# Constants in two loads, vectors loaded by ScalarE, gate rows dealt over the tiles, and conv rows and squares ahead in the delta rule

## The reference, cut to what matters

```
mk, mv = rmsnorm(mem) @ w_ck, rmsnorm(mem) @ w_cv            # 256 x 2048 each
proj = rmsnorm(x) @ w_in          # [q | k | v | z_A | alpha | beta | u | z_B]
q, k, v = silu(short_conv(proj[qkv], width 4)); q, k = l2norm(q) / sqrt(128), l2norm(k)
beta, g = sigmoid(..), -exp(a_log) * softplus(alpha + dt_bias)
o, state = gated_delta_rule(q, k, v, g, beta)                # 8 heads of 128, chunked
o_a = rmsnorm(o) * silu(z_A);  o_b = pooling(u) * silu(z_B)
x = x + [o_a, o_b] @ w_out
x = x + attention(rmsnorm(x) @ w_cq, mk, mv) @ w_co;  y = rmsnorm(x)
```

## Time and profile before

| | us |
|---|---|
| runs | 1755.1 median, 1754.63 to 1756.45 (3 runs) |
| the profiled execution's own time | 1756.3 |
| its span | 1754.5 |
| TensorE busy | 1698.6 (97%) |
| VectorE, ScalarE, GpSimd busy | 767.5, 604.8, 145.8 |
| DMA | 225.06 MB, mean 128 GB/s |

### The profile page before, as it was taken

The page is one execution under the profiler, slowest core; times in us unless marked ns, Lnnn a source line. Parts: engine busy times, 40 slices in busy tenths (PEclk is TensorE's granted clock), DMA queues, the critical chain, the costliest instruction groups (busy, mean ns, idle before and its releaser), DMA issues.

```text
span 1754.5 us, 31473 instructions
## 1 busy us (share of the span) xinstructions
PE 1698.6 (97%) x13184; PEld 1573.0 (90%) x13184; DVE 767.5 (44%) x1296; ACT 604.8 (34%) x967; POOL 145.8 (8%) x159
## 2 busy tenths in 40 slices
PE   5999999999999999999999999999999999999997
PEld 4887898998989998999999999999999987499997
DVE  4666435756646556465333343233122143422222
ACT  4565433442543434425322222222212133322222
POOL 0000000121111111211100001111000000000110
PEclk9999999999999999999999999999999999999999
DMA  6787643231332332414233334444433386723422
GB/s 228 235 290 240 202 110 84 71 105 52 109 87 73 86 84 74 110 49 122 66 93 92 81 99 148 129 128 143 151 91 96 100 329 267 222 75 108 121 79 103
DMA packets 272251, 225.06 MB, mean 128 GB/s; under 512 B 9785, under 2 KB 238914, under 8 KB 266706
## 3 DMA queue, kind: packets, MB, share of 16 engines
q1 hardware_dynamic: 272178, 224.03, 41.9%
HBM read 199.07 MB, written 25.30 MB: 128 GB/s over the span
## 4 chain that ended last, share of the span: by engine, by line
PE 92%; ACT 3%; issue 2%; DMA 1%; DVE 1%; POOL 0%; SPq 0%; ACTq 0%; DVEq 0%; POOLq 0%
PE pj L273 64%; PE pj L437 10%; PE dk L2140 2%; PE pj L2159 1%; PE dk L353 1%; PE dk L2071 1%; PE dk L1155 1%; PE pj L2082 1%; PE dk L1690 1%; PE pj L2168 1%; PE dk L1161 1%; PE dk L726 1%; PE dk L1299 1%; PE dk L1320 1%; DMA out_dram<-yb 1%
## 5 line engine op out<-in xcount | busy, mean ns | idle before, releaser
L273 PE MATMUL pj<-a_hi,w_high 128*128 128x272 f32 x2560 | 552.8, 297 | 12.6 <-ACT st L868 6.6
L273 PE MATMUL pj<-a_hi,w_low 128*128 128x272 f32 x2560 | 530.0, 288 | 0.0
L273 PE MATMUL pj<-a_lo,w_high 128*128 128x272 f32 x2560 | 528.4, 288 | 0.0
L273 PEld LDWEIGHTS pj<-a_hi,w_high 128*128 128x128 f32 x2560 | 402.4, 189 | 26.6 <-issue 21.1
L273 PEld LDWEIGHTS pj<-a_lo,w_high 128*128 128x128 f32 x2560 | 402.8, 189 | 0.0
L273 PEld LDWEIGHTS pj<-a_hi,w_low 128*128 128x128 f32 x2560 | 400.4, 189 | 0.0
L257 DVE TENSOR_TENSOR w_low<-w_raw,w_high 128x2048 fp32r<-128x2048 f32 x96 | 219.8, 2289 | 360.7 <-ACT w_high L247 360.6
L247 ACT ACTIVATE w_high<-w_raw 128x2048 fp32r<-128x2048 f32 x96 | 183.3, 1910 | 52.2 <-PE pj L273 44.8
L273 PE MATMUL pj<-mix_lo,w_high 128*128 128x272 f32 x512 | 105.7, 287 | 0.0
L273 PE MATMUL pj<-mix_hi,w_high 128*128 128x272 f32 x512 | 105.7, 288 | 0.0
L273 PE MATMUL pj<-mix_hi,w_low 128*128 128x272 f32 x512 | 105.6, 287 | 0.0
(11 more groups left out here) (394 smaller groups left out, 1797.7 us busy)
## 6 DMA issues: line engine op xcount, KB each, us to landing
w_raw<-in_w_in_dram SPq DMA_DIRECT2D x48, 1024.0 KB, 6.0
w_raw_wide<-in_w_ck_dram SPq DMA_DIRECT2D x16, 1024.0 KB, 6.6
w_raw_wide<-in_w_cv_dram SPq DMA_DIRECT2D x16, 1024.0 KB, 5.7
w_raw<-in_w_out_dram SPq DMA_DIRECT2D x16, 1024.0 KB, 6.0
w_raw<-in_w_cq_dram SPq DMA_DIRECT2D x16, 1024.0 KB, 5.9
w_raw<-in_w_co_dram SPq DMA_DIRECT2D x16, 1024.0 KB, 6.1
xr<-xT_scratch SPq DMA_DIRECT2D x16, 272.0 KB, 6.3
x2T_scratch<-x SPq DMA_DIRECT2D x16, 272.0 KB, 5.4
```

The lines of the kernel that those rows point to most:

```text
L273: mm = pe.matmul(pj[:, 2 * (q % 2) + b, 0:n], wt[:, k, :], x(k, o, n), start=(k == 0 and m == 0), stop=(k == KT - 1 and m == 2))
```

## The change

The constants are laid out anew, so that the identity and two columns of biases (NFIRST = 136 columns) come first; they are one load, and the rest, without columns of its own for the biases, a second one behind the first weight tile. The seven vector loads are issued by ACT, behind its table load. In group 0 of stage mem bank 2 is turned ahead of the products, banks 3 to 7 at earlier units, cast and split of part 1 go ahead of taking banks 2 and 3, and ACT's casts of parts 2 and 3 go between the two banks of their part. The gate rows' products stand after step 9; part 1 moves from q = 0 to q = 1 on ACT and DVE. In act_delta the square is two instructions with a signal each, k's part first, which the norms wait for one by one; `zraw` is taken behind the squares and not at the end of the head before; `rows()` of q = 2 stands ahead of the level-64 copies.

```diff
-C_ID, C_ONE, C_INCL, C_OWN, C_UP = 0, 128, 256, 384, 416
+C_ID, C_EPS, C_LNQ, C_ONE, C_INCL, C_OWN, C_UP = 0, 128, 129, 136, 264, 392, 424
+NFIRST = C_ONE
...
         def sp_mem(sp):
             sp.dma_start(xin[0][:], t["mem_prompt"][0, 0:P, :]).then_inc(x_loaded, 16)
-            sp.dma_start(cst[:], t["consts"][:, 0:NCONST]).then_inc(const_loaded, 16)
+            sp.dma_start(cst[:, 0:NFIRST], t["consts"][:, 0:NFIRST]).then_inc(const_loaded, 16)
             sp.dma_start(xin[1][:], t["mem_prompt"][0, P:MEM, :]).then_inc(mem1_loaded, 16)
-            for name, o, n in (("norm_mem", G_MEM, 16), ("norm_mix", G_MIX, 16), ("norm_cross", G_CROSS, 16),
...
-            sp.dma_start(vrow[0:NCONV, 1, :], t["conv_w"].rearrange("o j (k p) -> (o j k) p", p=P)).then_inc(vec_loaded, 16)
             for q in range(3):
                 sp.dma_start(raw_wide[q][:], source("mem", 0, q)).then_inc(w_loaded[q], 16)
+                if q == 0:
+                    sp.dma_start(cst[:, NFIRST:NCONST], t["consts"][:, NFIRST:NCONST]).then_inc(ab_loaded, 16)
...
             turn_mem(1)(pe)
+            turn_mem(2)(pe)
...
-                        if q < 3:
-                            steps = {2: [turn_mem(2 * q + 2)], 7: [turn_mem(2 * q + 3)]}
+                        steps = ({1: [turn_mem(3)], 7: [turn_mem(4)]}, {1: [turn_mem(5)], 6: [turn_mem(6)]},
+                                 {1: [turn_mem(7)]}, {})[q]
...
         def act_mem(act):
             act.preload_act_table_set("sqrt_and_others")
+            for name, o, n in (("norm_mem", G_MEM, 16), ("norm_mix", G_MIX, 16), ("norm_cross", G_CROSS, 16),
...
+            act.dma_start(vrow[0:NCONV, 1, :], t["conv_w"].rearrange("o j (k p) -> (o j k) p", p=P)).then_inc(vec_loaded, 16)
...
+                    if j == 0 and 0 < q < 3:
+                        take_mem(2 * q + 2)
+                    cast_high(act, "mem", j, q + 1)
+                    if j == 0 and q == 0:
+                        take_mem(2)
                     if j == 0 and q < 3:
-                        take_mem(2 * q + 2)
                         take_mem(2 * q + 3)
-                    cast_high(act, "mem", j, q + 1)
...
-                    if j == 0 and q < 3:
+                    if j == 0 and 0 < q < 3:
                         take_mem(2 * q + 2)
                         take_mem(2 * q + 3)
                     split_low(dve, "mem", j, q + 1)
+                    if j == 0 and q == 0:
+                        take_mem(2)
+                        take_mem(3)
...
-            pool.wait_ge(ab_loaded, 48)
+            pool.wait_ge(ab_loaded, 64)
...
-                act.activation(SQ[:], kq[:, 0:2], ACT.Square).then_inc(sq_done, 1)
+                for r in (1, 0):
+                    act.activation(SQ[:, r], kq[:, r], ACT.Square).then_inc(sq_done, 1)
+                act_take(act, n, 3)
...
+                rows()
                 act.wait_ge(p1_done, NLEV * n + 3)
...
                 act.activation(uu[0:2 * T32, :, 2 * T32:4 * T32], tiles32(1, 2 * T32)[0:2 * T32], ACT.Copy).then_inc(u_next, 1)
-                rows()
...
             def norms(pe):
-                pe.wait_ge(sq_done, n + 1)
...
-                for i in range(4):
+                for i in (2, 3, 0, 1):
+                    if i % 2 == 0:
+                        pe.wait_ge(sq_done, 2 * n + 2 - i // 2)
...
-                    if is_first(h) or q != 1:
+                    if q != 3 and (is_first(h) or q != 1):
                         act_take(act, h, q)
...
-            for part in ((0, 1), (), (2,), ())[q]:
+            for part in ((0,), (1,), (2,), ())[q]:
                 act_rows(act, part)
...
-                        for part in ((0, 1), (), (2,), (3,))[q]:
+                        for part in ((0,), (1,), (2,), (3,))[q]:
                             dve_rows(dve, part)
...
-                steps = delta_steps(h - 1) if not is_first(h) else [{5: [pe_rows]}, {}, {}, {4: [pe_cols]}]
+                steps = delta_steps(h - 1) if not is_first(h) else [{9: [pe_rows]}, {}, {}, {4: [pe_cols]}]
```

More of the change, by code:

```diff
@@ L69 @@
 C_INV = C_BM + NB
-C_EPS = C_INV + NG * 16
-C_LNQ = C_EPS + 1
-NCONST = C_EPS + 2
+NCONST = C_INV + NG * 16
 C_REQ = NCONST
@@ L380, in sp_mem @@
             sp.dma_start(xin[0][:], t["mem_prompt"][0, 0:P, :]).then_inc(x_loaded, 16)
-            sp.dma_start(cst[:], t["consts"][:, 0:NCONST]).then_inc(const_loaded, 16)
+            sp.dma_start(cst[:, 0:NFIRST], t["consts"][:, 0:NFIRST]).then_inc(const_loaded, 16)
             sp.dma_start(xin[1][:], t["mem_prompt"][0, P:MEM, :]).then_inc(mem1_loaded, 16)
-            for name, o, n in (("norm_mem", G_MEM, 16), ("norm_mix", G_MIX, 16), ("norm_cross", G_CROSS, 16),
-                               ("norm_final", G_FINAL, 16), ("gdn_norm", G_GDN, 1), ("pool_scale", G_POOL, 8)):
-                src = t[name].rearrange("(o n) -> o n", o=1) if name == "norm_final" else t[name]
-                sp.dma_start(vrow[o:o + n, 0, :], src.rearrange("o (k p) -> (o k) p", p=P)).then_inc(vec_loaded, 16)
-            sp.dma_start(vrow[0:NCONV, 1, :], t["conv_w"].rearrange("o j (k p) -> (o j k) p", p=P)).then_inc(vec_loaded, 16)
             for q in range(3):
                 sp.dma_start(raw_wide[q][:], source("mem", 0, q)).then_inc(w_loaded[q], 16)
+                if q == 0:
+                    sp.dma_start(cst[:, NFIRST:NCONST], t["consts"][:, NFIRST:NCONST]).then_inc(ab_loaded, 16)
             sp.wait_ge(x_scaled, 1)
@@ L519, in act_mem @@
             act.preload_act_table_set("sqrt_and_others")
+            for name, o, n in (("norm_mem", G_MEM, 16), ("norm_mix", G_MIX, 16), ("norm_cross", G_CROSS, 16),
+                               ("norm_final", G_FINAL, 16), ("gdn_norm", G_GDN, 1), ("pool_scale", G_POOL, 8)):
+                src = t[name].rearrange("(o n) -> o n", o=1) if name == "norm_final" else t[name]
+                act.dma_start(vrow[o:o + n, 0, :], src.rearrange("o (k p) -> (o k) p", p=P)).then_inc(vec_loaded, 16)
+            act.dma_start(vrow[0:NCONV, 1, :], t["conv_w"].rearrange("o j (k p) -> (o j k) p", p=P)).then_inc(vec_loaded, 16)
             x_stats(act, 0, xin[0], P)
@@ L1997, in build @@
         kct_a = Reused(p1_ready, 3 * HEADS)
-        svr_a = Reused(sq_done, HEADS)
+        svr_a = Reused(sq_done, 2 * HEADS)
         qm_ready = Reused(lt_ready, HEADS)
```

## The result

The kernel after takes 1741.75 us (median of 4 runs, 1741.5 to 1742.96); the kernel before, run beside it, 1754.95 (4 runs, 1754.63 to 1756.45). The ratio is 0.9923, 95% interval 0.9912 to 0.9935: 13.2 us faster, where 14.2 were forecast. The profiled execution has a time of 1742.96 and a span of 1741.1, 13.4 less than before's.

What follows compares the result with a forecast made beforehand. TensorE, busy for 97% of the span, was taken to bound the kernel, so only its waits or clock pay. 5.3 + 1.1 + 6.6 + 1.2 = 14.2 us less gave 1740.9 us (1741), range 1737 to 1745.5.

Steps and rivals of the forecast that it cites:

- Opening, first half: Opening: fewer constants ahead of ACT's second memory block, so it lands 0.9 us earlier; bounds 0 and 1.1.
- Opening, second half: Group 0: new order of casts and banks removes three 1.27 us waits, 3.8 us, plus 0.6 us of transposes.
- Rival (b): Opening gives the load's gain alone: 9.8 us in all instead of 14.2, 1745.3 us; chance 0.12.
- Gate rows: Head 0: waits of 2.47 and 4.20 us go, a new 6.7 us wait comes inside tile 2; net 1.1 us.
- Rival (c): Dealing the rows really empties head 0: both waits vanish, 9.6 us, 1732.4 us; chance 0.04.
- Fourth tile's wait: Heads: TensorE's wait for ACT's conv rows at the fourth product tile goes, 6.6 us in all; bounds 5.2 and 7.4.
- Rival (d): Slower: conv rows wait for late transposes and hold level-64 pair and fourth tile in seven heads; 1767 us; chance 0.02.
- Squares: Heads 1 to 7: norms' 0.8 us wait goes, most reappears ahead of gram; 0.17 us a head, 1.2 in all.
- Rival (a): Norms' gain passes in full in seven heads: 5.6 us instead of 1.2, 1736.5 us; chance 0.10.

## Why the prediction was right

**The sum.** 14.2 us were forecast, 13.4 by the profiled spans and 13.2 by the medians came. At the last gram 14.99 are there, 0.8 more than the sum: 5.27 for 5.3 in the opening, 1.47 for 1.1 in head 0, 8.25 for 7.8 in the heads. Of the 1.8 given back from co on, 1.5 are its clock, which no term of mine held. The terms are right in their mechanisms, save for one step in the first, but that the total is off by 1 us only is partly luck: differences of either sign cancelled, within the opening too.

**Opening, first half.** The one term that failed: "so the block lands 0.9 us earlier". It was 0.14 in the profile compared and 0.6 on average. The bytes taken out did what was worked out for them, as 0.89 us less pass from the first block to the second. Wrong was that a late first block is one "which the second block's chain does not feel": it came 0.66 us later (6.42 for 5.76; 0.29 on average), within the bound of 1 us that was given, and the second, on which the first product hangs, came later with it. I had not looked for a scatter, having one profile; the first block's is 5.73 to 6.09 us in the seven profiles with SP's vectors and 5.76 to 6.42 in the seven with ScalarE's.

**Opening, second half.** Right in its mechanism: no wait for a cast, part 3 at 39.09 where 39.0 stood. Its terms were too small by what the load's was too large: 1.27 us of idle before a part were worth 1.59, 1.53 and 2.01, the last with a turn of four transposes, worth 0.48 where the recorded 0.60 was taken. Rival (b), the load alone, falls by the kernel with the order alone.

**Gate rows.** Right step by step. On before's clock (the times of after plus 5.27 us) part 1 on VectorE was to run from 260.3 to 276.4 and ran from 259.8 to 275.9; the wait of 6.7 was 6.68 and the clock behind it 0.50; tile 3 was to start at 285.7 and started at 285.27. L734 had no wait. The net was 1.6 us at tile 3 for 1.1 (285.27 for 286.85), 1.47 at the gram, and 0.85 there with this part alone. Rival (c) falls; what it takes to empty head 0 is shown by the two kernels that reorder VectorE.

**Fourth tile's wait.** 6.6 forecast, 6.94 measured alone. Rival (d) needed transposes 2.1 us late; in the kernel after, the transposes of a steady head end at 475.77, ScalarE's two copies run from 475.81 to 476.23, and the level-64 copy starts at 477.17, not delayed:

```profile
475.81 0.27 ACT L875 ACTIVATE st<-pj 3x128 f32<-3x128 f32 x1 [0.45 <-PE pj L869]
...
477.17 0.38 ACT L966 ACTIVATE s<-dk 64x256 f32<-64x256 f32 x1 [0.93 <-PE dk L1259]
```

With this part alone a head became shorter by all of the wait (1.01 for 0.97).

**Squares.** 1.2 forecast, 1.27 measured, and the wait of 0.8 a head back as 0.57 in front of the gram. Rival (a), the full 5.6, falls, by the kernel with this part alone and by after. The reason given, the chain cast, split, kq, is confirmed by moving the cast.

## What to carry to other kernels

When a wait is removed, look at once for the input that comes next and how late it is: 0.30 us of slack behind a wait of 0.8 capped the gain at 0.2 a head. If the two inputs hang on one engine's order, move the piece that feeds the second one too: the cast alone gave nothing, the squares alone 1.3 us, the cast on top of them another 5.6. And move long vector work that nobody waits for soon (the rows' scan, 16 us) behind, or around, the short piece that somebody does.

## What the hardware showed unexpectedly

**A wait costs more than the idle time shown.** Removing 0.57 us of idle a head gave 0.83, removing 1.27 in the opening 1.53. The rows say why: a pair's record lasts 0.41 us while the next pair starts 0.25 later, so a stall also loses an overlap of 0.16, and what follows it is longer (eight gram products 1.99 us behind the wait, 1.89 without; a pair in the opening 0.70 for 0.61). Together some 0.25, which fits both. At the fourth tile, 0.97 us of idle were worth only 1.01; what makes that one cheaper no run settles.

**TensorE's full speed comes at a different moment in each execution.** In the opening the first pairs of 512 columns take 1.05 to 1.2 us, then 0.62; over fourteen profiles the change falls between 20.30 and 23.85 us, also with the same first product (17.63 and 17.60: at 20.89 and 23.62). With the order of after, the way from the first product to part 3 takes 20.17 us where full speed came 3.3 us after the first product, and 21.56 where it came 6.0 after, so it is worth up to 1.4 us, more than the term for the load. The profile's granted clock doesn't show it: it reads 1.00 in 17.7:20.0 of after, where the pairs take twice their time. The rows of after:

```profile
22.93 0.80 PE L433 MATMUL pj<-w_high_wide,hm_lo 128*128 128x512 f32 x2
...
23.57 0.62 PE L433 MATMUL pj<-w_high_wide,hm_hi 128*128 128x512 f32 x2
```

So steps of 1 us in this kernel are read between markers of the timeline (from the first gram to the last, executions with the same order agree within 0.2 us) and not from medians.
